# Two-layer decoder trunk: where layer 2's first condition part is fetched and on which engine it is summed

## The reference

```python
cond = jax.nn.silu(c)
for l in range(DEPTH):
    mod = (cond @ w_ada[l] + b_ada[l])[:, None, :]
    sh1, sc1, g1, sh2, sc2, g2 = jnp.split(mod, 6, axis=-1)
    h = x * (1.0 + sc1) + sh1
    u, q_lat, kv_lat, k_rope = jnp.split(h @ w_in[l], split_cols, axis=-1)
    pooled = causal_pool_mixer(u, w_pool[l], pool_scale[l])
    attn = mla_mixer(q_lat, kv_lat, k_rope, ...)
    mixed = jnp.concatenate([pooled, attn], axis=-1) @ w_out[l]
    x = layer_norm(DEEPNORM_ALPHA * x + g1 * mixed, ln1_g[l], ln1_b[l])
    h = x * (1.0 + sc2) + sh2
    ffn = swiglu(h, shared expert) + routed_moe(h, 64 experts, top 8)
    x = layer_norm(DEEPNORM_ALPHA * x + g2 * ffn, ln2_g[l], ln2_b[l])
```

## Time and profile before

| | |
|---|---|
| median of 3 runs | 1308.72 us (1307.75 to 1309.2) |
| the profiled execution's own time | 1308.44 us |
| its span, first to last instruction | 1306.7 us |
| PE busy | 1228.8 us, 94% of the span |
| PEld busy | 772.2 us, 59% |
| DVE busy | 511.3 us, 39% |
| ACT busy | 249.8 us, 19% |
| POOL busy | 160.8 us, 12% |
| mean transfer rate | 379 GB/s |
| chain that ended last | PE 81%, DMA 8%, DVE 6% |

### The profile page before, as it was taken

The page is one execution under the profiler, slowest core; times in us unless marked ns, Lnnn a source line. Parts: engine busy times, 40 slices in busy tenths (PEclk is TensorE's granted clock), DMA queues, the critical chain, the costliest instruction groups (busy, mean ns, idle before and its releaser), DMA issues.

```text
span 1306.7 us, 28004 instructions
## 1 busy us (share of the span) xinstructions
PE 1228.8 (94%) x9286; PEld 772.2 (59%) x9286; DVE 511.3 (39%) x1119; ACT 249.8 (19%) x518; POOL 160.8 (12%) x587
## 2 busy tenths in 40 slices
PE   6998999999799999999988899999979999999995
PEld 3474566666366666566646557666646665566563
DVE  5675842222222233223387555222222322133335
ACT  1222211111111111111223312111111111111113
POOL 1000022111111111111000002111111111011110
PEclk9999999999899999999989899999999999899998
DMA  9999979999999999999998356999999999989992
GB/s 316 389 408 392 402 294 421 420 421 421 421 421 421 420 422 420 397 395 402 418 342 344 147 228 251 420 379 422 421 421 420 421 421 422 420 350 393 393 408 103
DMA packets 83920, 494.87 MB, mean 379 GB/s; under 512 B 11969, under 2 KB 20193, under 8 KB 29057
## 3 DMA queue, kind: packets, MB, share of 16 engines
q1 hardware_dynamic: 83842, 493.71, 92.9%
HBM read 492.60 MB, written 1.08 MB: 378 GB/s over the span
## 4 chain that ended last, share of the span: by engine, by line
PE 81%; DMA 8%; DVE 6%; SPq 3%; issue 2%; ACT 1%; DVEq 0%; ACTq 0%
PE ps L1054 30%; PE ps L1076 15%; PE ps L985 9%; PE ps L1097 7%; DMA ring<-in_w_exp_gate 5%; PE ps L995 4%; PE ps L907 3%; DMA ring<-in_w_ada 2%; PE ps L935 2%; PE ps L710 2%; SPq L505 1%; PE ps L1026 1%; DMA w<-in_w_ada 1%; PE ps L1069 1%; DVE acc L1428 1%
## 5 line engine op out<-in xcount | busy, mean ns | idle before, releaser
L1054 PE MATMUL ps<-ring,w 128*64 128x256 f32 (+1 forms) x3648 | 413.9, 385 | 0.4
L1054 PEld LDWEIGHTS ps<-ring,w 128*64 128x64 f32 (+1 forms) x3648 | 259.1, 127 | 68.6 <-issue 14.2
L1076 PE MATMUL ps<-ring,w 128*64 128x512 f32 (+1 forms) x912 | 207.7, 597 | 0.0
L1054 PE MATMUL ps<-flex,w 128*32 128x256 f32 x736 | 170.9, 392 | 26.5 <-DMA ring<-in_w_exp_gate 17.7
L1718 DVE SCALAR_TENSOR_TENSOR w<-ps,w 128x256 f32<-128x256 f32 x57 | 27.6, 484 | 373.8 <-PE ps L1054 373.8
L1054 PE MATMUL ps<-w 128*32 128x256 f32 x736 | 171.4, 393 | 0.0
L1704 DVE CAST scat<-ps 128x512 fp32r<-128x512 f32 x114 | 78.9, 692 | 158.9 <-PE ps L1076 158.9
L985 PE MATMUL ps<-hx,scat 128*128 128x512 f32 x472 | 138.2, 417 | 0.7 <-issue 0.7
L1054 PEld LDWEIGHTS ps<-flex,w 128*32 128x32 f32 x736 | 81.4, 113 | 85.5 <-issue 43.7
L1234 ACT ACTIVATE w<-ps 128x512 f32<-128x512 f32 x118 | 70.6, 598 | 291.7 <-PE ps L985 291.7
L1097 PE MATMUL ps<-scat 128*128 128x512 f32 x456 | 119.1, 403 | 0.0
(11 more groups left out here) (265 smaller groups left out, 1278.9 us busy)
## 6 DMA issues: line engine op xcount, KB each, us to landing
ring<-in_w_exp_gate SPq DMA_DIRECT2D x88, 1024.0 KB, 18.9
ring<-in_w_exp_up SPq DMA_DIRECT2D x88, 1024.0 KB, 22.4
ring<-in_w_exp_down SPq DMA_DIRECT2D x88, 1024.0 KB, 22.0
ring<-in_w_ada SPq DMA_DIRECT2D x30, 1024.0 KB, 11.6
w<-in_w_exp_gate SPq DMA_DIRECT2D x20, 1024.0 KB, 16.5
w<-in_w_exp_up SPq DMA_DIRECT2D x20, 1024.0 KB, 18.7
flex<-in_w_exp_gate SPq DMA_DIRECT2D x20, 1024.0 KB, 13.5
flex<-in_w_exp_up SPq DMA_DIRECT2D x20, 1024.0 KB, 15.4
```

The source lines that it names most:

```text
L1054: last = mm(ps[unit * g:unit * g + unit, bank, 0:F], hTb[:, kt, unit * g:unit * g + unit], weights(k)[:, kt, :], start=kt == 0, stop=kt == ...
L1076: last = mm(ps[unit * g:unit * g + unit, bank, :], midT[:, f, unit * g:unit * g + unit], down_w(k)[:, f, half * 512:(half + 1) * 512], sta ...
```

## The change

SP fetches the eight tiles of layer 2's part 0 no longer in layer 1's attention but at the end of layer 1's loop, into the parts of slots 0, 1 and 4 that the last four-slot round has finished with: three tiles after its gate projections, two (and w_in's last piece) after its up projections, three after its down projections. TensorE multiplies each tile by the condition (32 equal columns, four column groups) into bank 6, starting from the bias; ScalarE copies the result, TensorE turns it into columns, VectorE makes modl between its two normalisations. Everything of this in layer 1 goes, and so does SP's wait for scores_done. Behind it, layer 2's part 1 is fetched as a whole after the sum (next_used), before w_uq, w_pool and w_ukv, and part 2's last four tiles move ahead of w_out.

```diff
-ADA_JOBS = ((None, 0, 8), (None, 24, 32))
-NEXT_JOB = 16
+ADA_JOBS = ((None, 0, 8), (None, 16, 24))
...
+        next_at = [part_w(slot, part * KT * F, KT * F)
+                   for slot, part in ((0, 0), (1, 0), (4, 0), (0, 1), (1, 1), (0, 2), (1, 2), (4, 1))]
...
             def next_tiles(kts):
                 for kt in kts:
-                    n = NEXT_JOB + kt
-                    sp.wait_ge(ada_used[n % ADA_BUFS], n // ADA_BUFS + 1)
                     src = w_ada[1:2, kt * P:(kt + 1) * P, 0:ADA_W]
-                    sp.dma_start(ada_at[n % ADA_BUFS], src.rearrange("a p n -> p (a n)")).then_inc(ada_landed[n % ADA_BUFS], 16)
+                    sp.dma_start(next_at[kt], src.rearrange("a p n -> p (a n)")).then_inc(p0_landed[kt], 16)
...
                     quads, used = btab_value(sp, NROUNDS - 1), btab_value(sp, NROUNDS)
+                    sp.wait_ge(s["gate_done"], quads)
+                    next_tiles((0, 1, 2))
+                    sp.wait_ge(s["gu_done"], quads)
+                    next_tiles((3, 4))
+                    load_w_in(1, 5, 8, 3)
                     sp.wait_ge(s["down_done"], quads * 2)
-                    load_w_in(1, 5, 8, 3)
-                    ada_tiles(1, 1, (0, 1, 2, 3))
-                    load_ukv(1)
+                    next_tiles((5, 6, 7))
                     sp.wait_ge(s["gath_done"], (used + 1) * 2)
                     load_w_in(1, 0, 3, 0)
                     load_w_in(1, 3, 5, 1)
                     sp.wait_ge(s["layer_ready"], 1)
+                    vectors(1)
+                    sp.dma_start(band_sb, band_dram).then_inc(s["band_in"], 16)
+                    sp.wait_ge(s["next_used"], KT)
+                    ada_tiles(1, 1, range(KT))
+                    load_uq(1)
+                    load_pool(1)
+                    load_ukv(1)
                     ada_bias(1, 1)
                     ada_bias(1, 2)
-                    vectors(1)
-                    sp.dma_start(band_sb, band_dram).then_inc(s["band_in"], 16)
-                    load_uq(1)
-                    load_pool(1)
-                    ada_tiles(1, 1, (4, 5, 6, 7))
                     ada_tiles(1, 2, (0, 1, 2, 3))
...
+                else:
+                    ada_tiles(1, 2, (4, 5, 6, 7))
                 load_w_out(0, 4)
                 load_w_out(4, 8)
                 if l == 0:
                     ada_tiles(0, 1, (6, 7))
                     ada_tiles(0, 2, (0, 1, 2, 3))
-                else:
-                    ada_tiles(1, 2, (4, 5, 6, 7))
...
-                sp.wait_ge(s["scores_done"], (l + 1) * H)
-                if l == 0:
-                    sp.wait_ge(s["acc0_zeroed"], 2)
-                    sp.dma_start(acc0[0:1, :], b_ada[1:2, 0:ADA_W]).then_inc(s["acc0_bias_in"], 16)
-                    next_tiles((0, 1, 2, 3))
                 store_mod(l, 1)
                 store_mod(l, 2)
-                if l == 0:
-                    next_tiles((4,))
...
-                if l == 0:
-                    next_tiles((5, 6, 7))
...
                 sp.wait_ge(s["table_ready"], l + 2)
+                if l == 0:
+                    sp.dma_start(acc0[0:1, :], b_ada[1:2, 0:ADA_W]).then_inc(s["acc0_bias_in"], 16)
```

TensorE, front of layer 2:

```diff
+                    pe.wait_ge(s["acc0_bias_in"], 48)
+                    for g in range(4):
+                        mm(ps[32 * g:32 * g + 32, NEXT_BANK, :], ones[0:1, 0:32], acc0[0:1, g * 512:(g + 1) * 512],
+                           start=True, stop=False)
+                    for kt in range(KT):
+                        pe.wait_ge(p0_landed[kt], 48)
+                        for g in range(4):
+                            last = mm(ps[32 * g:32 * g + 32, NEXT_BANK, :], c32v[:, kt, :], next_at[kt][:, g * 512:(g + 1) * 512],
+                                      start=False, stop=kt == KT - 1)
+                        last.then_inc(s["next_used"], 1)
+                    pe.wait_ge(s["next_copied"], 1)
+                    for i in range(4):
+                        last = mm(ps[:, NEXT_BANK, i:2 * KT:4], acc0[:, i * P:(i + 1) * P], one_of_4, start=True, stop=True)
+                    last.then_inc(s["p0_columns"], 1)
                     turn_x2(0)
```

TensorE, layer 1:

```diff
-                if l == 0:
-                    pe.wait_ge(s["p0_done"], CHUNKS + 1)
-                    for g in range(4):
-                        last = mm(ps[32 * g:32 * g + 32, 0, :], ones[:, 0:32], acc0[:, g * 512:(g + 1) * 512], start=True, stop=True)
-                    last.then_inc(s["p0_summed"], 1)
...
-                if l == 0:
-                    for i in range(4):
-                        last = mm(ps[:, 1, P0_COL + i:P0_COL + 2 * KT:4], acc0[:, i * P:(i + 1) * P], one_of_4, start=True, stop=True)
-                    last.then_inc(s["p0_columns"], 1)
```

ScalarE, front of layer 2:

```diff
+                        if j == 0:
+                            act.wait_ge(s["next_used"], KT)
+                            fn(acc0[:, 0:512], ps[:, NEXT_BANK, :], ACT.Copy).then_inc(s["next_copied"], 1)
                         act.wait_ge(s["modl_ready"], CHUNKS + 1)
```

VectorE, layer 1:

```diff
-                    next_part(range(5))
...
-                    next_part((5, 6, 7))
-                    dve.sem_inc(s["p0_done"], 1)
...
-                    dve.wait_ge(s["p0_summed"], 1)
-                    v.tensor_copy(acc0[:, 0:512], ps[:, 0, :])
```

VectorE, front of layer 2:

```diff
                     for j in range(NT):
                         norm_stats(j, None)
                         normalise(j, NT + j + 1).then_inc(s["n2_ready"], 1)
+                        if j == 0:
+                            dve.wait_ge(s["p0_columns"], CHUNKS + 1)
+                            shift, scale = (ps[:, NEXT_BANK, a:a + KT] for a in (0, KT))
+                            v.scalar_tensor_tensor(modl[:, KT:2 * KT], scale, 1.0, g2_col, ALU.add, ALU.mult)
+                            link(v.scalar_tensor_tensor(b2_col, scale, 1.0, b2_col, ALU.add, ALU.mult))
+                            v.tensor_tensor(modl[:, 0:KT], shift, b2_col, ALU.add).then_inc(s["modl_ready"], 1)
```

More of the change, by code:

```diff
@@ L363, in decoder_trunk @@
         B_F, B_T, B_0, B_1 = 4, 5, 6, 7
-        P0_COL = 448
+        NEXT_BANK = 6
         names = """consts_in x_in c_in pos_in eps_set cT_done c32_ready bias_in mod_val_ready acc0_zeroed acc0_bias_in mod1_summed
@@ L372, in decoder_trunk @@
         rows1_in rows2_in ln_stats ln_std cols_in t_ready h2A_ready h2D_ready first_link gates_ready table_warm
-        back_done order_read bias_zeroed p0_summed otab_ready x1_ready x2_ready sum2_ready nmu2_ready var2_ready
+        back_done order_read bias_zeroed next_used next_copied otab_ready x1_ready x2_ready sum2_ready nmu2_ready var2_ready
         std2_ready part2_ready h2T_done router_in rbias_in logits_done esc_ready sh_up_done R_ready shsil_ready
@@ L517, in _ @@
                     quads, used = btab_value(sp, NROUNDS - 1), btab_value(sp, NROUNDS)
+                    sp.wait_ge(s["gate_done"], quads)
+                    passed(sp)
+                    next_tiles((0, 1, 2))
+                    sp.wait_ge(s["gu_done"], quads)
+                    passed(sp)
+                    next_tiles((3, 4))
+                    load_w_in(1, 5, 8, 3)
                     sp.wait_ge(s["down_done"], quads * 2)
                     passed(sp)
-                    load_w_in(1, 5, 8, 3)
-                    ada_tiles(1, 1, (0, 1, 2, 3))
-                    load_ukv(1)
+                    next_tiles((5, 6, 7))
                     sp.wait_ge(s["gath_done"], (used + 1) * 2)
@@ L584, in _ @@
                 sp.dma_start(down_w(3), lay(w_sh_down, l).rearrange("a (k p) d -> p (a k) d", p=P)).then_inc(s["sh_landed"], 16)
-                if l == 0:
[L586 to L590, removed]
+                for n in range(ADA_JOBS[l][2] + 4, ADA_JOBS[l][2] + 7):
+                    sp.wait_ge(ada_used[n % ADA_BUFS], n // ADA_BUFS + 2)
                 for half in range(2):
@@ L1020, in _ @@
                         turned(b0)
-                        pe.wait_ge(s["modl_ready"], CHUNKS + 1)
                         pe.wait_ge(s["order_read"], l + 1)
@@ L1297, in _ @@
                     pool.wait_ge(s["layer_ready"], l)
+                    pool.wait_ge(s["next_used"], KT)
                     passed(pool)
@@ L1300, in _ @@
                 eng.memset(mod_bias[2], 0.0).then_inc(s["bias_zeroed"], 1)
-                if l == 0:
-                    pool.wait_ge(s["mod1_summed"], 1)
-                    eng.memset(acc0[:, :], 0.0).then_inc(s["acc0_zeroed"], 1)
                 first = B0 if l == 0 else last
@@ L1428, in summed_part @@
                             ins = v.scalar_tensor_tensor(acc, tile, c32v[:, kt, 0:1], acc, ALU.mult, ALU.add)
-                        ins.then_inc(ada_used[buf], 1)
-                        dve.wait_ge(ada_used[buf], n // ADA_BUFS + 2)
-                def next_part(kts):
-                    for kt in kts:
-                        n = NEXT_JOB + kt
-                        buf = n % ADA_BUFS
-                        dve.wait_ge(ada_landed[buf], (n // ADA_BUFS + 1) * 16)
```

(10 more changed lines are left out.)

## The result

| kernel | median us (lowest to highest, runs) | ratio to the kernel before, 95% interval |
|---|---|---|
| before | 1308.14 (1306.16 to 1309.48, 12) | 1 |
| changed | 1309.69 (1307.14 to 1313.44, 12) | 1.0017 (1.0009 to 1.0025) |

The change makes the kernel 0.17% slower by the medians. The interval leaves out "no change" by little, and the difference of 1.55 us is smaller than the 2.6 us that the prediction set as what can be told; the forecast was 1310.3 us. The profiled execution is the fastest of the twelve (1307.14 us, span 1305.3), so its rows are read stretch by stretch and not by its end.

The account below looks back on a forecast made before the run. TensorE's chain was taken to bound 81% of the span, with the transfer queue full in both expert loops. Terms -3.1 + 11.2 - 5.1 - 1.1 = +1.9 us gave 1310.3 us, own range 1308.5 to 1311.3, wider range 1306.4 to 1313.6.

Parts of the forecast that it names:

- Layer 1's tail, -3.1: End of layer 1's attention: removing sums, column sums and column matmuls starts the loop 3.1 us earlier (1.32 + 0.99 + 0.8).
- The 8 MB taken off the queue there give nothing: Layer 1's attention: fewer transfers gain nothing, since the loop's late weights wait for the expert order behind an empty queue.
- The seam, +11.2: Layer 1's loop end to layer 2: the new tiles and the chain behind them delay the first projection 11.2 us.
- Landing and tile price: Seam: each new tile costs 2.5 us and w_in's piece 3.5, so the last new tile lands at 665.9.
- The steps behind it: Seam, after the last tile: matmuls 1.94 us, ScalarE's copy 0.75, columns 1.7, transposes to first projection 1.6.
- The 0.7 us that I gave back: Layer 2's first projection: TensorE, longer at work by then, avoids the half-speed start, saving 0.7 us.
- Part 2 ahead of w_out, -5.1: Layer 2's scores: VectorE no longer waits for a tile behind w_out, TensorE sets the start, 5.1 us come back.
- the clock behind the scores, -1.1: After layer 2's scores: TensorE goes on without its wait, so two sums avoid the low clock, winning 1.1 us.
- Low clock all through: Rival: every step behind the last tile at low clock, seam 12.4, 1.1 not won; +4.2 us, 1312.9; chance 0.2.
- Part 2 late: Rival: part 2's first tile comes late behind w_uq, w_pool, w_ukv, margin 0.9 us; +3 to +7 us; chance 0.18.
- Shorter seam: Rival: full clock throughout the seam, delay 9.0 us, so +0 us, 1308.4; chance 0.17.
- faster loop: Rival: TensorE's waits in layer 1's loop shrink as the stream gains more lead; 1304 us at 6; chance 0.1.

Follow-up runs that it names:

- Experiment 9: The kernel before with VectorE's eight layer 1 sums of part 0 narrowed from 2048 columns to one; only rows used, 68.3 us from mix to loop.
- experiment 2: The kernel before with only part 2's last four tiles moved ahead of w_out; 1302.45 us, ratio 0.9961.
- 7: The kernel before with part 2's last four tiles ahead of w_out and 13 narrow constant matmuls in TensorE's wait at layer 2's front; 1301.37 us.
- 4: The changed kernel plus 13 constant matmuls, 512 columns wide, in TensorE's waits for the new tiles; 1311.04 us, ratio 1.0031.
- Experiment 5: The changed kernel plus 13 constant matmuls, 256 columns wide, in TensorE's waits for the new tiles; 1306.55 us, ratio 0.9987.
- 6: The changed kernel with w_in's first piece behind the new tiles and 13 constant matmuls, 256 columns wide, in the waits; 1305.94 us, ratio 0.9983.
- experiment 3: The changed kernel with w_in's first piece behind the last three new tiles instead of ahead of them; 1305.14 us, ratio 0.9985.
- 8: The changed kernel with only the first four of the eight new tiles fetched and summed; only rows used, seam 7.92 us.
- experiment 1: The changed kernel with w_out put back ahead of part 2's last four tiles; 1318.82 us, ratio 1.0082.
- 10: The changed kernel with w_in's first piece behind the new tiles and 2, 2, 1 narrow constant matmuls behind the last three; 1305.20 us, ratio 0.9976.
- 11: 10 with part 1's first four tiles ahead of vectors and band, its last four behind w_uq, w_pool and w_ukv; 1312.82 us, ratio 1.0039.

## Why the prediction came out

The time was right: 1310.3 forecast, 1309.69 measured, inside the forecast's own range. Of its terms one was clearly off, layer 1's gain, which was some 1.1 us larger than forecast. That the total agrees better than this is partly luck: most executions probably lost more in the seam than the profiled one did.

**Layer 1's tail, -3.1: too small, and one step wrong.** The issue of the late weights moved by 5.25 us in the profile. Over the table, the ten kernels without part 0 in layer 1 start the loop at 179.59 to 183.35, the three with the whole sums at 185.25 to 185.65: 4.1 less on average, and N is 4.2 less. The step that failed is "The 8 MB taken off the queue there give nothing". Experiment 9 shows that these transfers, more than the sums, hold VectorE until 130.8; what that costs TensorE is estimated there and not measured. Without them the loop starts 66.5 us after the mix, and the mix begins anywhere from 113.1 to 116.9, depending on when layer 1's own last tiles land and on the clock behind that wait: in 104 to 108 us it was 1.00 in the kernels whose mix began at 113.12 to 114.52, and 0.50 to 0.63 in those at 115.35 to 116.88. With the sums TensorE waits for VectorE the longer, the earlier the mix begins: 1.32 us in the kernel before (the wait of the earlier trace rows, from the latest of these three mixes), 2.16 in 2 and 2.22 in 7. That these three start the loop within 0.4 us of one another is in part an accident. In 7 TensorE's transposes begin 1.6 us earlier than in the kernel before, but behind the wait the clock was 0.81 in 137 to 146, and the mix's last 16 instructions took 8.73 instead of 7.03 us:

```profile
136.21 1.16 PE L917 MATMUL ps<-const,flex 128*128 128x128 f32 x8 [2.22 <-DVE flex L1560]
137.20 8.73 PE L908 MATMUL ps<-w,flex 128*128 128x512 f32 x16
```

That the loop keeps most of a lead won before the expert order was right.

**The seam, +11.2: right in size, wrong in a part.** The first projection came 9.9 us later against N, and took 1.0 more (11.59 against 10.60): +10.9. Landing and tile price were right: 13.0 us from N to the last tile, 13.7 forecast. The steps behind it took 4.7 us and not 6.0, since columns and transposes ran at the full clock in this execution. The 0.7 us that I gave back for the clock in the projection were a loss of 1.0 (clock 0.50 in 666 to 668); experiments 4 to 7 put the projection at full clock at 9.90. Experiments 3 and 8 confirm that the last tile's landing sets the seam.

**Part 2 ahead of w_out, -5.1, and the clock behind the scores, -1.1: right.** VectorE's start on the scores against N moved by +6.2, so 4.7 of the 10.9 came back, and the mix by +5.0, so 1.2 more; L698 takes 1.06 instead of 1.94. Alone, in the kernel before, both together bring 5.3 to 5.7 (experiment 2). In the changed kernel undoing them costs more, 9.1, which the prediction did not ask: its own moves put w_out and these tiles later.

**The sum.** -4.2 (mean of N) + 10.9 - 4.7 - 1.2 = +0.8 us at layer 2's mix, against +1.55 between the medians. The difference fits the clock, though this is argued and not shown: the changed kernel's profile was of its fastest execution, and the one of experiment 1, with the same order of transfers in the seam, ran 1.5 us longer there. The profiled span is 1.4 us under that of before although the mix is 0.5 later; what follows that mix, which the change leaves alone, was 1.9 shorter in it. Why was not tried.

**The rivals.** Low clock all through is half true. In the changed kernel the clock stood at 0.50 in 656 to 660, behind a wait of 2.95 us and between tiles. The rule of the Trainium skill (page "TensorE: Matmul & The Clock Gate", section "HAM oscillation — how this bites in real kernels"), that a tile starts cold where the matmuls before it were shorter than the wait for it, agrees with the traces in part. In experiment 3 the last tile's matmuls, behind a wait of 1.41 us that was longer than the 1.07 us of the tile before, took 1.07 us at a granted clock of 1.00 (656 to 660); the clock fell only after them, to 0.50 in 662 to 666. In experiment 1 a tile behind a wait of 2.85 us took 1.06 us. Experiment 5 prices the low clock at 3.1 us of the median; but the 1.1 us behind the scores were won all the same, so the sum stayed under 1312.9 (which adds the 4.2 to the median; added to 1308.44, as in the forecast, they give 1312.6). Part 2 late: the margin, put at 0.9 us, was used up, and VectorE waited 0.29; it was longer, 1.21, 1.75 and 3.07 us, in experiments 5, 6 and 10, where the projection took only 9.90 us. Shorter seam and faster loop did not come. The gain of layer 1 was larger than forecast for another reason than the rival's.

## What to carry to other kernels

Split a change of several moves before judging it: here one line of the queue's order, worth 5 us alone, hid the cost of the rest. A wait read from one execution is a sample: where two chains race, look at several executions before one of them is called the bound, since the start of layer 1's mix alone varied by 3.8 us. Where TensorE idled before work on the critical path, matmuls on constants kept the clock up for free when they were shorter than the wait (experiments 5 and 7), and delayed the work when they were longer (4 and 6). In 10 they cost no more than 0.4 us at the last tile, and the time still did not fall: by its rows VectorE's late sums then set the pace.

## What was not expected of the hardware

SP's issue of a transfer can itself take microseconds. In the changed kernel two of the new tiles and a vector of 1 KB took this long to issue; two tiles of the same kind took 0.98 us at 619.11:

```profile
628.63 7.40 SPq L438 DMA_DIRECT2D ring<-in_w_ada  x2
...
650.43 6.88 SPq L475 DMA_DIRECT2D colv<-in_kv_norm_g  x1
```

All of these long issues fall where several transfers issued before them had not landed. That SP waits for room in the queue is argued from this and not shown: there were unlanded transfers at 619.11 too, and the tiles issued quickly there landed only 20 to 22 us later.

A small transfer of no urgency, issued there ahead of a large one, can delay it by more than its bytes: in 10 the next tiles are issued 3.8 us after the last new tile's matmuls, behind the vectors and the band, and in 11, ahead of them, 0.1 us after.
